# VectorE's weight splits one chunk later in the last unit of mixer A, and the last sums of squares one split earlier in the first unit

## The reference

```python
h = rmsnorm(x, norm_g)                       # needs mean(x*x) over 2048 per token
proj = einsum('bsd,de->bse', h, w_in)        # q, k, v, gate of both mixers
ya = chunk_relbias_attention(aq, ak, av, rel_bias) * silu(ag)   # mixer A: 16 heads of 64
yb = swa_sink_gqa(rope(bq), rope(bk), bv, sinks) * silu(bg)     # mixer B: 16 heads, 2 kv heads
x  = x + einsum('bse,ed->bsd', concat([ya, yb]), w_out)
```

## Time and profile before

| | before |
|---|---|
| median of 3 runs | 1622.51 us (1622.07 to 1624.85) |
| the profiled execution | 1622.79 us, its span 1620.2 us |
| TensorE matmul busy | 1595.9 us, 99% of the span |
| TensorE's mean granted clock | 0.994 of full speed |
| VectorE busy | 1244.2 us, 77% |
| ScalarE busy | 932.0 us, 58% |
| GpSimd busy | 420.6 us, 26% |

### The profile page before, as it was taken

One profiled execution on the slowest core, in us unless ns is written; L12 is line 12 of the kernel. 1 busy time (PEld: TensorE's weight loads), 2 busy tenths in 40 slices (PEclk: granted clock), 3 DMA queues, 4 the chain that ended last, 5 costly groups with the idle time before them and its releaser, 6 DMA issues.

```text
span 1620.2 us, 28427 instructions
## 1 busy us (share of the span) xinstructions
PE 1595.9 (99%) x9289; PEld 1409.6 (87%) x9289; DVE 1244.2 (77%) x2619; ACT 932.0 (58%) x1969; POOL 420.6 (26%) x554
## 2 busy tenths in 40 slices
PE   9999999999999999999999999999999999999997
PEld 7889989989788888899988998999987888888997
DVE  7787777787567777888877778777775777888874
ACT  7666656656456666433466666666655566664333
POOL 1544353342122210000144335345312321000000
PEclk9999999999999999999999999999999999999998
DMA  6233323333422232344432333333342323223443
GB/s 234 85 103 97 103 90 103 103 103 109 141 94 92 91 111 92 98 156 156 164 117 79 104 104 102 96 94 106 103 155 92 98 94 111 83 91 118 131 143 117
DMA packets 77510, 180.68 MB, mean 112 GB/s; under 512 B 9408, under 2 KB 13792, under 8 KB 70640
## 3 DMA queue, kind: packets, MB, share of 16 engines
q1 hardware_dynamic: 76960, 178.99, 34.0%
q10 hardware_dynamic: 432, 0.55, 0.1%
q0 software_dynamic: 32, 0.08, 0.0%
HBM read 163.25 MB, written 11.62 MB: 108 GB/s over the span
## 4 chain that ended last, share of the span: by engine, by line
PE 90%; DVE 4%; issue 2%; ACT 2%; POOL 1%; DMA 1%; DVEq 0%; SPq 0%; POOLq 0%; ACTq 0%
PE ps_proj L719 9%; PE ps_proj L721 9%; PE ps_proj L720 9%; PE ps_proj L895 3%; PE ps_proj L894 3%; PE ps_proj L896 3%; PE ps_proj L881 3%; PE ps_proj L883 3%; PE ps_proj L882 3%; PE ps_o L789 2%; PE ps_t L776 2%; PE ps_s L881 2%; PE ps_s L883 2%; PE ps_s L882 2%; PE ps_s L894 2%
## 5 line engine op out<-in xcount | busy, mean ns | idle before, releaser
L1562 DVE TENSOR_TENSOR w_lo<-w_raw,w_hi 128x512 fp32r<-128x512 f32 (+1 forms) x528 | 446.4, 853 | 96.5 <-ACT w_hi L1099 91.9
L1099 ACT ACTIVATE w_hi<-w_raw 128x512 fp32r<-128x512 f32 (+1 forms) x528 | 377.9, 725 | 190.9 <-DVE w_raw L1931 66.0
L719 PE MATMUL ps_proj<-act_hi,w_hi 128*128 128x512 f32 x704 | 277.7, 394 | 0.0
L720 PE MATMUL ps_proj<-act_lo,w_hi 128*128 128x512 f32 x704 | 275.4, 391 | 0.0
L721 PE MATMUL ps_proj<-act_hi,w_lo 128*128 128x512 f32 x704 | 275.1, 391 | 0.0
L2258 POOL TENSOR_TENSOR w_raw<-w_raw 128x128 f32<-128x128 f32 x112 | 73.8, 659 | 363.7 <-DMA w_raw<-w 363.7
L1164 ACT ACTIVATE probs<-probs,nmax 128x128 f32<-128x128 f32 (+3 forms) x128 | 72.1, 564 | 148.6 <-DVE nmax L1634 148.6
L721 PEld LDWEIGHTS ps_proj<-act_hi,w_lo 128*128 128x128 f32 x704 | 132.6, 188 | 28.7
L1099 ACT ACTIVATE arena<-ps_t 128x512 fp32r<-128x512 f32 (+4 forms) x168 | 74.8, 450 | 138.7 <-PE ps_t L776 88.0
L719 PEld LDWEIGHTS ps_proj<-act_hi,w_hi 128*128 128x128 f32 x704 | 132.7, 189 | 24.7
L720 PEld LDWEIGHTS ps_proj<-act_lo,w_hi 128*128 128x128 f32 x704 | 132.8, 189 | 24.4
(11 more groups left out here) (376 smaller groups left out, 4482.9 us busy)
## 6 DMA issues: line engine op xcount, KB each, us to landing
w_raw<-w SPq DMA_DIRECT2D x322, 256.0 KB, 3.0
w_raw<-w SPq DMA_DIRECT2D x51, 1024.0 KB, 4.9
temp<-temp SPq DMA_DIRECT2D x72, 64.0 KB, 4.1
strips_tables<-ext SPq DMA_DIRECT2D x16, 256.0 KB, 4.2
temp<-xT SPq DMA_DIRECT2D x16, 256.0 KB, 4.4
xs<-xy SPq DMA_DIRECT2D x16, 256.0 KB, 4.4
temp<-xs SPq DMA_DIRECT2D x16, 256.0 KB, 4.1
strips_tables<-ext SPq DMA_DIRECT2D x16, 224.0 KB, 4.5
```

Of the source, the lines that this page charges most:

```text
L719: pe.matmul(dst, wh, act_hi[:, k, :], start=start, stop=False)
L720: pe.matmul(dst, wh, act_lo[:, k, :], start=False, stop=False)
L1099: return nc.scalar.activation(dst, src, ACT.Copy, scale=scale)
L1562: return nc.vector.tensor_tensor(dst, src, hi, ALU.subtract)
```

## The change

Two edits, both in VectorE's program. In `unit`, VectorE splits each chunk one point later than before, so that it takes the chunk that ScalarE copied at the point before; the fourth chunk of the unit's first tile moves from ahead of point 0 into it, and the last chunk comes behind point 15. In the first unit of each layer `presum_squares` moves from point 10 to point 9, ahead of the split of tile 3's second chunk. No instruction is added or taken away.

```diff
             def unit(T, L, att, ab, nxt):
-                for c in range(LO_AHEAD, PTS):
+                for c in range(LO_AHEAD, PTS - 1):
                     lo_next(T, c)
                 for s in range(4):
                     for pt in range(PTS):
                         p = s * PTS + pt
-                        attend(att, p, L, ab, ab, lambda: split_w(T, s + 1, pt))
+
+                        def other():
+                            if p == 0:
+                                lo_next(T, PTS - 1)
+                            else:
+                                split_w(T, (p - 1) // PTS + 1, (p - 1) % PTS)
+                        attend(att, p, L, ab, ab, other)
...
                         duties(T, L, p, nxt)
+                split_w(T, 4, PTS - 1)
...
-                        if p == 2 * PTS + 2:
+                        if p == 2 * PTS + 1:
                             presum_squares(L)
```

## The result

| | before | after |
|---|---|---|
| median | 1623.23 us (1622.07 to 1624.85, 4 runs) | 1612.35 us (1611.45 to 1613.97, 4 runs) |
| ratio to before, 95% interval | | 0.9931 [0.9916, 0.9945] |
| the profiled execution, its span | 1622.79, 1620.2 us | 1612.97, 1611.0 us |
| TensorE's mean granted clock | 0.994 | 0.996 |

The changed kernel is 10.9 us faster by the medians and 9.8 us by the two profiled executions. It lies 0.35 us from the forecast of 1612.0.

What follows compares the result with a forecast made beforehand. TensorE, busy 99%, loses time only to waits for VectorE and its lower clock. Edit 1's 9.1 us plus edit 2's 1.0 and 0.5 make 10.6 us, giving 1612.0 us; range 1609.5 to 1616.5.

Steps and rivals of the forecast that it cites:

- six waits: Mixer A's two last units: TensorE's transposes wait for VectorE's low part, 4.1 and 3.3 us; all were to go.
- path of four splits: Layer 0's last unit: four splits leave the path ahead of the 2.34 us wait, 4 x 0.69 = 2.8 us.
- The clock loss of 1.7 us: Behind layer 0's last-unit wait of 2.34 us: 3.4 us at the lower clock, 1.7 us lost, to be regained.
- short waits: Mixer A's last units: two further waits per layer, 1.8 and 1.0 us in sum, taken as gone too.
- The wait at the spread: Layer 0's first unit, L1028: a new TensorE wait of 2.3 us in place of the 3.0 us one.
- the time of the copy: Layer 0's first unit: ScalarE's copy, needed by VectorE's next split, ends at 40.94 + 0.61 = 41.55.
- Its last sentence: Signs of a wrong forecast, among them a clock falling in the new wait and costing over edit 2's 1.0 us.
- the moved wait: Layer 0's first unit: the mean square's 3.0 us wait, moved to the spread as 2.3 us.
- Only the long waits go: Rival, chance 0.21: short waits in mixer A's last units stay or come back; 7.8 us gained, 1614.7, up to 1617.
- The last unit hardly changes: Rival, chance 0.04: mixer A's last-unit path runs through ScalarE's queue alone; only edit 2's 1.5 us, 1621.
- The rope late by the fetch: Rival, chance 0.03: mixer B's third rope swap lies behind SyncE's 4.9 us fetch; 13.8 us slower, 1625.8.

Runs made afterwards that it cites:

- e3: Kernel before with only the start of mixer A's last units changed: the fourth low part formed inside point 0, no later splits; 1618.06 us, ratio 0.9966.
- e4: Changed kernel with the fourth low part ahead of the loop again, no split at point 0, sums of squares in their old place; 1612.57 us, ratio 0.9926.
- e2: Kernel before with the second edit alone (last sums of squares ahead of a split in each layer's first unit); 1622.56 us, ratio 0.9989.
- e1: Changed kernel with the sums of squares back in their old place, so the first edit alone; 1613.09 us, ratio 0.9933.
- e12: The changed kernel itself, unaltered, timed and profiled once more; 1612.10 us, ratio 0.9931.
- e6: Changed kernel with SyncE's last 1 MB fetch of the unit held until just ahead of the third rope's swap; 1613.99 us, ratio 0.9943.
- e8: Changed kernel with the second pair of block-sum low parts behind the spread roots (point 12, not 11) in each layer's first unit; 1612.67 us, ratio 0.9934.
- e10: Changed kernel, work left out: low parts for the next unit's first weight chunks cover 2 columns in each layer's first unit; 1610.57 us, ratio 0.9918.

## Why the prediction was right

**Edit 1: right, sized 1.1 us too low.** Forecast 9.1 us, measured 10.16 us in the profile. All six waits went. The forecast took the waits at their listed lengths, 4.1 and 3.3 us; the rows above show that the list leaves out about 0.16 us in each, 1.0 us in six. With that, layer 0 is 4.1 + 0.5 + 1.6 = 6.2 (measured 6.28) and layer 1 is 3.3 + 0.5 = 3.8 (3.88). The term that was mis-sized is thus the length of the six waits. The same sum gives e3's units within 0.1 us: its waits of 3.2 and 2.2 us, with 0.5 each and without a fall, make 61.0 and 60.0 of 57.32. The forecast's path of four splits, with one at the start, was more than was needed: e4 leaves the start as it was and loses nothing. The clock loss of 1.7 us was taken from one window; e2 priced it at 1.6. The same wait brought it on in three of the four last units profiled with it (before: layer 0; e2: both), so the medians, 10.9 us apart, may hold more of it than the two profiles, which have it once; no run shows how much. That the short waits would go was a close call in the forecast, though it did not say so: it took 1.3 us off each low part, and the longest of the short waits was 1.26 us.

**Edit 2: the mechanism right, the sizes nearly.** The sums now end at 37.94, ahead of TensorE. They take 0.69 and 1.04 us. The forecast had 2.35 for both from the earlier trace rows; the first is 0.52 us shorter here, the second is as long as before. What moved the reciprocal is another term, the split ahead of it (third line):

```profile
36.11 0.69 DVE L2012 TENSOR_TENSOR temp<-temp 128x512 f32<-128x512 f32 x1
36.90 1.04 DVE L2015 TENSOR_TENSOR temp<-temp 128x512 f32<-128x512 f32 x1
...
41.16 0.69 DVE L1562 TENSOR_TENSOR w_lo<-w_raw,w_hi 128x512 fp32r<-128x512 f32 x1 [2.08 <-ACT w_hi L1099]
...
44.06 0.17 DVE L2041 RECIPROCAL r_cols<-r_cols 128x4 f32<-128x4 f32 x1
```

The wait at the spread came, 1.8 us for 2.3 forecast, with the reciprocal at 44.06, which is 0.96 us earlier than before counted from the split of 35.50 (0.5 forecast). The forecast had the time of the copy right: by it the split could start 5.6 us behind the split of 35.50, and it started 5.66 us behind. But from its start to the reciprocal it is 2.90 us and not 3.41, since this split takes 0.69 us where the one of the earlier trace rows took 1.21. From the reciprocal to the first transposes it was 21.48 us; I had taken 20.84 from layer 1. The two errors of about half a microsecond cancel, and that is luck: 0.85 us against the forecast's 1.0, and 0.43 against its 0.5 in layer 1. The size also depends on the execution that one compares with. From the split to the first transposes the kernels with the old order took 30.48 us (e1, e3), 30.89 (before) and 31.21 (e4), the longer the later the clock was back, and the changed kernel 30.04: layer 0's gain is 0.4 to 1.2 us.

**What the forecast named but did not price.** Its last sentence warned of a clock that falls behind the moved wait and costs more than 1.0 us. In the profile of the changed kernel it did, 2.2 us, and not behind the spread but behind the first transposes, where TensorE now stands for 1.75 us; in e12 it did not. This is the step that the forecast lacked, a term of 2.2 us that it put at nothing: it gave a length for the wait at the spread and none for the one at the transposes, though its own numbers held one: TensorE, no longer slowed from 42 to 48 us, is there earlier than VectorE's chain.

**The sum.** 9.1 + 1.0 + 0.5 = 10.6 us forecast. In the two profiles 10.16 + 0.85 + 0.43 - 2.2 = 9.2 us of span, with stretches on both sides of these places evening out (0.4 earlier at the start, 0.5 later behind layer 0's last unit). In e12, without the fall, the span is 10.5 us under that of before. So the way to the forecast's 10.6 us is the one that it describes, but that the median of 1612.35 us lies only 0.35 us from 1612.0 is in part luck: edit 1 gave 1.1 us more than forecast, and the fall that was not priced takes 2.2 us back in some executions.

**The rivals.** Only the long waits go: no, the short ones went too. The last unit hardly changes: no. The rope late by the fetch: it has 2.4 us of slack now, up from 0.99, as VectorE's chain to that tile is shorter; even forced behind the fetch (e6) it costs TensorE at most 0.3 us in one layer's unit.

## What to carry to other kernels

Where one engine makes the high part and another the low part of the same chunk, let the second work one chunk behind the first: its waits for a copy inside a chain that TensorE waits for then go (here from over 1 us each to 0.36 us at one split). One chunk was enough; the lag comes back as work behind the loop, and a second chunk cost 1.3 us in the profile and gave nothing. A wait that is removed by earlier work on a nearly full engine mostly moves (here 3.0 us of wait with its fall of the clock was worth 0.4 to 1.2 us): ask for the next place where TensorE needs that engine, and whether the clock holds behind the longer wait there.

## What the runs showed of the hardware

- A wait of the same length brings TensorE's clock down in one execution and not in the next. Behind 1.71 to 1.75 us at the first transposes it fell in two of five profiles, behind 2.29 and 2.31 in both, behind 1.47 and less in none of six; behind 2.33 to 2.34 us in the last units in three of four. Behind the spread's wait of 1.8 us it fell in one of eight (e8). These are counts in single profiles; what decides between the executions is not shown. A fall cost 1.3 to 2.2 us where its stretch can be compared with one that kept the clock.
- Beside GpSimd's additions VectorE's subtraction of 128x512 took 1.2 us in the earlier trace rows, and 0.69 us in the changed kernel at 41.16. There it was GpSimd's addition beside it (from 41.27) that was long, 1.19 us where those before it at 39.75 and 40.45 took 0.74. An estimate of a VectorE chain beside GpSimd has this 0.5 us of doubt in each instruction.
- A subtraction of 128x2 still takes 0.15 to 0.41 us (e10), where one of 128x512 takes 0.69.
- Matmuls of 128x512 at the full clock start 0.23 us apart and are drawn 0.39 us long, so a listed wait of TensorE is some 0.16 us too short; e3's two units bear this out to within 0.1 us.
